# Two-map attention: no products of constants on TensorE, ScalarE's copy ahead of the next exponentials, a second pair of masked score tiles

## The reference, cut to what matters

```python
for l in range(DEPTH):                      # DEPTH = 2
    u = rmsnorm(x, norm1_g[l]) @ w_in[l]
    y_m = mlstm_mixer(...)                  # gated recurrence, all steps as one matrix
    y_a = diff_attention(...)               # the two-map attention
    y_h = hgrn2_mixer(...)                  # a second recurrence
    x = x + concat([y_m, y_a, y_h]) @ w_out[l]
    x = x + square(relu(rmsnorm(x, norm2_g[l]) @ w_up[l])) @ w_down[l]

def block(args):                            # 128 queries of the two-map attention
    s = einsum('bhcqd,bhckd->bhcqk', qi, kt)        # c: the two maps
    mask = qpos[:, None] >= kpos[None, :]
    p = softmax(where(mask, s, NEG_BIG), axis=-1)
    a = p[:, :, 0] - lam * p[:, :, 1]
    return einsum('bhqk,bhkv->bhqv', a, v)
```

## Time and profile before

| | |
|---|---|
| Median of 3 runs | 3468.72 us (3467.31 to 3468.8) |
| Profiled execution, its own time | 3470.07 us |
| Its span in the trace | 3468.3 us |
| Mean granted TensorE clock | 0.994 of full |
| TensorE matmul busy | 3410.0 us (98%) |
| VectorE busy | 1393.4 us (40%) |
| ScalarE busy | 1012.3 us (29%) |
| GpSimd busy | 1510.3 us (44%) |

### The profile page before, as it was taken

The page is one execution under the profiler, slowest core; times in us unless marked ns, Lnnn a source line. Parts: engine busy times, 40 slices in busy tenths (PEclk is TensorE's granted clock), DMA queues, the critical chain, the costliest instruction groups (busy, mean ns, idle before and its releaser), DMA issues.

```text
span 3468.3 us, 41846 instructions
## 1 busy us (share of the span) xinstructions
PE 3410.0 (98%) x16720; PEld 2748.6 (79%) x16720; DVE 1393.4 (40%) x2596; ACT 1012.3 (29%) x1275; POOL 1510.3 (44%) x522
## 2 busy tenths in 40 slices
PE   8999999899999999999999999999999999999999
PEld 7878878588888888886888887877888878778887
DVE  6565248735253524136312126854101158541010
ACT  2222322622223212224322233443212234442121
POOL 3545552035455545540354564502645545025453
PEclk9999999999999999999999999999999999999999
DMA  7444222024353443212222222201222212012222
GB/s 281 181 155 182 102 85 74 1 104 188 139 191 119 183 150 142 95 49 69 73 86 102 90 99 73 74 25 49 97 97 97 97 68 79 25 49 97 96 96 75
DMA packets 58748, 358.65 MB, mean 103 GB/s; under 512 B 10208, under 2 KB 10592, under 8 KB 21856
## 3 DMA queue, kind: packets, MB, share of 16 engines
q1 hardware_dynamic: 58592, 356.50, 28.6%
HBM read 354.38 MB, written 2.10 MB: 103 GB/s over the span
## 4 chain that ended last, share of the span: by engine, by line
PE 94%; DVE 3%; ACT 1%; issue 1%; DMA 1%; SPq 0%; POOL 0%; DVEq 0%; ACTq 0%
PE LP L572 85%; PE XB L572 8%; ACT E L1351 1%; DMA big<-w_ada 1%; PE LP L950 0%; PE XB L795 0%; DVE XB L2068 0%; PE XB L831 0%; ACT sq L1351 0%; DVE big L2248 0%; DVE big L2250 0%; DVE S L2424 0%; DVE big L2247 0%; DVE u L2909 0%; DVE h L2315 0%
## 5 line engine op out<-in xcount | busy, mean ns | idle before, releaser
L1855 POOL TENSOR_TENSOR w_lo<-ring,w_hi 128x2048 fp32r<-128x2048 f32 (+3 forms) x275 | 1134.4, 4125 | 700.0 <-ACT w_hi L1351 699.8
L572 PE MATMUL LP<-u_hi,w_hi 128*128 128x512 f32 x2448 | 959.5, 392 | 2.6 <-ACT u_hi L1351 2.4
L572 PE MATMUL LP<-u_hi,w_lo 128*128 128x512 f32 x2448 | 954.4, 390 | 0.0
L572 PE MATMUL LP<-u_lo,w_hi 128*128 128x512 f32 x2448 | 934.9, 391 | 0.0
L572 PE MATMUL LP<-big_r,w_hi 128*128 128x512 f32 x2520 | 780.3, 390 | 4.9 <-DVE h L2315 2.5
L1351 ACT ACTIVATE w_hi<-ring 128x2048 fp32r<-128x2048 f32 (+3 forms) x275 | 474.4, 1725 | 749.7 <-PE LP L572 746.8
L572 PE MATMUL LP<-big_r,w_lo 128*128 128x512 f32 x1508 | 587.5, 390 | 0.0
L572 PEld LDWEIGHTS LP<-big_r,w_hi 128*128 128x128 f32 x2520 | 472.6, 188 | 106.1 <-DVE h L2315 4.2
L572 PEld LDWEIGHTS LP<-u_hi,w_hi 128*128 128x128 f32 x2448 | 460.5, 188 | 111.6 <-issue 16.1
L572 PEld LDWEIGHTS LP<-u_lo,w_hi 128*128 128x128 f32 x2448 | 462.4, 189 | 96.2 <-issue 0.5
L572 PEld LDWEIGHTS LP<-u_hi,w_lo 128*128 128x128 f32 x2448 | 460.5, 188 | 95.8
(11 more groups left out here) (353 smaller groups left out, 3497.6 us busy)
## 6 DMA issues: line engine op xcount, KB each, us to landing
ada_in<-w_ada SPq DMA_DIRECT2D x66, 1024.0 KB, 4.9
ring<-w_in SPq DMA_DIRECT2D x20, 1024.0 KB, 4.8
ring<-w_gu00a SPq DMA_DIRECT2D x11, 1024.0 KB, 7.1
ring<-w_gu00b SPq DMA_DIRECT2D x11, 1024.0 KB, 6.6
ring<-w_gu01a SPq DMA_DIRECT2D x11, 1024.0 KB, 6.6
ring<-w_gu01b SPq DMA_DIRECT2D x11, 1024.0 KB, 6.7
ring<-w_gu10a SPq DMA_DIRECT2D x11, 1024.0 KB, 6.6
ring<-w_gu10b SPq DMA_DIRECT2D x11, 1024.0 KB, 4.9
```

Source lines behind the costliest of these rows:

```text
L572: return pe.matmul(o, lhsT=lhsT, rhs=rhs, start=start, stop=stop)
L1855: gp.tensor_tensor(w_lo[:, slab % RING, 0:width], ring[:, slab % RING, 0:width], w_high(q, width).bitcast(F32), ALU.subtract).then_inc(s(" ...
```

## The change

Four edits, all in the two-map attention.

- TensorE: `fill_heads` and its call go, 29 matmuls in each layer and their waits on `o_taken`.
- ScalarE: in step n the copy of unit n - 2 (`ET` from `XB[3]`) now stands ahead of the two exponentials of unit n. What `beside` does stays last.
- VectorE and ScalarE: odd units keep their masked scores in `big[:, HF:HF+2]` (two tiles that the recurrence has finished with) and not in `S`. So the mask of unit n waits for the exponentials of unit n - 2, not of unit n - 1.
- VectorE: one wait ahead of the pass, for its own last reads of `big[:, HF:HF+2]` (`x_ready`).

```diff
+        def diff_masked(n):
+            return big[:, HF:HF + 2, :] if n % 2 else S
...
-            def fill_heads(n, times):
-                if times and pl.head + n // NB > 1:
-                    pe.wait_ge(s("o_taken"), pl.head + n // NB - 1)
-                fill(times, LP[0][:, (pl.head + n // NB) % 2, :])
...
-                    fill_heads(n, {0: 5, 2: 5, 6: 2, 8: 2, 9: 3, 11: 2, 13: 3, 16: 5, 18: 2}.get(n, 0))
                     beside(n)
...
                 for n in range(n_units + 2):
+                    if n >= 2:
+                        i, W = n - 2, ((n - 2) % NB + 1) * P
+                        act.wait_ge(s("transposed"), p0 + i + 1)
+                        if i >= 2:
+                            act.wait_ge(s("pv_done"), p0 + i - 1)
+                        f(ET[:, i % 2, 0:W], XB[3][:, 0:W], ACT.Copy).then_inc(s("pt_done"), 1)
                     if n < n_units:
...
-                            f(E[:, k % 4, 0:W], S[:, m, 0:W], ACT.Exp, scale=-1.0, bias=stat[:, k % 4, 0:1],
+                            f(E[:, k % 4, 0:W], diff_masked(n)[:, m, 0:W], ACT.Exp, scale=-1.0, bias=stat[:, k % 4, 0:1],
                               accum_out=stat[:, k % 4, 1:2]).then_inc(s("diff_exp"), 1)
-                    if n >= 2:
-                        i, W = n - 2, ((n - 2) % NB + 1) * P
-                        act.wait_ge(s("transposed"), p0 + i + 1)
-                        if i >= 2:
-                            act.wait_ge(s("pv_done"), p0 + i - 1)
-                        f(ET[:, i % 2, 0:W], XB[3][:, 0:W], ACT.Copy).then_inc(s("pt_done"), 1)
                     beside(n)
...
-                            if n:
-                                dve.wait_ge(s("diff_exp"), u0 + k - 1)
+                            if n >= 2:
+                                dve.wait_ge(s("diff_exp"), u0 + k - 3)
                             dve.tensor_tensor_reduce(
-                                out=S[:, m, 0:W], in0=XB[k % 3][:, 0:W], in1=cc("causal", T - W, W), scale=1.0,
+                                out=diff_masked(n)[:, m, 0:W], in0=XB[k % 3][:, 0:W], in1=cc("causal", T - W, W), scale=1.0,
...
+                dve.wait_ge(s("x_ready"), 9 * (l + 1))
                 diff_attention(l, 2, st[:, 50 + l:51 + l], beside_maps)
```

## The result

The changed kernel takes 3479.99 us (median of 8 runs, 3475.69 to 3482.18) against 3468.76 before: ratio 1.0029, 95% interval 1.002 to 1.0039. It is slower by 11 us, clear of noise. It lies inside the range (3461 to 3482) but 7.5 us above the forecast, outside the forecast's own 3467 to 3478, and almost on case C's 3480.7.

What follows compares the result with a forecast made beforehand. TensorE, busy 98% of the span, was taken as the bound. Schedule -2.0 plus clock +3.9 gave +1.9 a pass, +3.8 in all: 3473.9 from the profiled execution, 3472.5 in terms of the runs' median; range 3461 to 3482.

Steps and rivals of the forecast that it cites:

- case C: Rival, slower: clock falls behind all five new spells, +8 a pass, ScalarE's queue passes it on; +12, 3480.7; chance 0.22.
- eight foretold waits: TensorE's idle spells in a pass once fills go: 1.75, 2.6, 0.66, 1.4, 1.57, 2.1, 1.9 and 2.85 us.
- n = 2: Second group of far products: TensorE idle 1.75 us for VectorE's copies, starting 2.95 us sooner than before.
- missing waits at n = 11 and 13: Sign against the forecast: TensorE should wait about 2 us each on ScalarE's gate copy there.
- "Nothing": Second pair of masked tiles: the freed wait ended last nowhere, so no gain; perhaps some tenths where ScalarE is late.
- The order of ScalarE: Exponentials of unit 9 behind the copy of unit 7 cost the queue to the gate copy 1.1 us.
- The gain of 0.4: n = 8: before, transposes waited 0.4 for a copy behind the exponentials of unit 7; the new order pays.
- Schedule alone: Waits without any clock effect: -2.0 us a pass, -4.0 in all, perhaps off by 1.5 a pass.
- The clock: Without fills, TensorE's clock falls three more times a pass at 1.3 us each: +3.9, between 0 and +8.
- is bound by TensorE again and moves with it: What follows the pass: no change of its own, it only shifts with the pass.
- B: Rival, the clock holds: spells under 2 us cost nothing, only the schedule counts; 3464.7, passes 59.7; chance 0.25.
- D: Rival, faster: new order and second tiles loosen the steps; 3455 with a steady clock, 3463 with falls; chance 0.08.

Runs made afterwards that it cites:

- experiment 1: The kernel before with its 29 products of constants a pass left out, nothing else changed: 3479.42 us, 1.0025 of before.
- changed kernel, fitted fills: The changed kernel given fills only as long as the wait each covers by the prediction's working: 3463.28 us, 0.9978 of before.
- fitted fills: The kernel before with fills resized to the waits of the prediction's working (none at n = 0, five at n = 4): 3463.96 us, 0.998 of before.
- the 3461 and 3463 kernels: Kernel before, resized fills, sums behind the pass spread among wide products, two fills there: 3461.19 us; resized fills alone in the kernel before, 3463.96, or changed kernel, 3463.28.

## Why the prediction was right or wrong, point by point

**The places and the releasers** were right in the main: of eight foretold waits (n = 2, 4, 6, 8, 9, 11, 13 and 16) the first pass has seven. At n = 11 it has none: TensorE, behind 10.2 us at half, was itself the last there. In the second pass, where that slow stretch is 6.8 us, the wait at n = 11 is there, 0.74 us. The prediction named missing waits at n = 11 and 13 as a sign that it is wrong; the first pass shows half of that sign. The sizes at 4, 6, 8, 9 and 16 were good to half a microsecond (2.14, 0.52, 1.47, 1.31 and 2.37); the two on the gate copy, forecast at 2.1 and 1.9, measured 0.74 at most and 0.80. The wait of 0.90 at n = 18, for ScalarE's copy, was not in the working.

**n = 2** was mis-sized: 2.88 us, not 1.75; the products start at t = 6.13, not 5.15. VectorE's second weights instruction took three times its length. Timelines of VectorE and of GpSimd:

```profile
2275.11 1.25 DVE L2396 SCALAR_TENSOR_TENSOR wk<-E,stat,wk 128x128 f32<-128x128 f32 x1
```

```profile
2274.95 1.26 POOL L2022 TENSOR_TENSOR Z<-Z,big 128x512 f32<-128x512 f32 x1
```

The Trainium skill (SBUF — State Buffer, "Who interferes with whom") has the rule: a VectorE instruction with two inputs in SBUF and a GpSimd instruction that reads SBUF share a port, and the later one waits for the whole of the other. The trace agrees: the instruction starts 0.16 us behind GpSimd's and ends 0.15 us behind it. Without fills and without the second pair of tiles (experiment 1) that instruction took 0.35 us, but the one ahead of it was held in its place. VectorE, GpSimd and TensorE there (the lines are numbered as in the kernel before):

```profile
2281.08 1.19 DVE L2396 TENSOR_SCALAR wk<-E,stat,st 128x128 f32<-128x128 f32 x1
```

```profile
2280.92 1.27 POOL L2025 TENSOR_TENSOR Z<-Z,big 128x512 f32<-128x512 f32 x1
```

```profile
2280.64 0.91 PE L572 MATMUL XB<-big 64*128 64x384 f32 x2 [0.62 <-DVE stat L2387]
...
2284.00 2.08 PE L572 MATMUL LP<-Z 64*128 64x256 f32 x8 [2.46 <-DVE wk L2856]
```

Behind a fill at n = 0 it takes 0.34. It reads one tile only, a case that the rule as told here does not cover. So the meeting with GpSimd's product comes with the missing fills at n = 0, not with the tiles. The tiles take away the wait of 0.62 us, and the products of n = 2 start at t = 6.13 with them and 6.45 without. "Nothing" was wrong for the tiles by 0.3 us a pass, a gain, in the kernels without a fill at n = 0 ("some tenths", as the prediction allowed), and right where the fills stand.

**The order of ScalarE**: the working gave it +1.1 us in the queue to the gate copy and a cost of about 1 us a pass. Measured 0.7 and 1.0 with all fills, and 1.3 at full clock with fitted ones, once the 0.31 of the tiles is counted apart. Right. The gain of 0.4 that I gave it at n = 8 isn't there: with the order alone the transposes still wait 0.4, for VectorE's weights.

**Schedule alone, -2.0 a pass**: 58.90 us at full clock (changed kernel, fitted fills) plus 1.5 for one slow stretch is 60.4, so -1.25. That is an estimate: no run has the changed kernel without fills at full clock. Off by 0.75, within the 1.5 allowed; the order and n = 2 are in it.

**The clock** is the term that was mis-sized. I took three more falls of 3.4 us each at 1.3, +3.9 a pass. The first pass has 27.3 us at half, 23.9 more than before, in five falls of 6.8, 3.4, 10.2, 3.4 and 3.4 us; the second has the same 27.3 in four. They cost 66.43 - 60.4 = +6.0. So there was more than twice the slow time that I had taken (10.2), and each 3.4 us of it cost less, 0.86 in place of 1.3. The link from waits to falls was wrong too. The wait of 2.37 at n = 16 has no fall behind it in the pass, and one fall begins with no wait near: from 2314.25 to 2317.70 TensorE is busy 3.38 of 3.45 us, on products of four rows among others, and then the clock is at half:

```profile
2314.25:2317.70 3.45, 3.38 (x12) 1.25 (x11) 3.19 (x9) 1.55 (x4) 0.00 (x0) 0.99 0.01 2
2317.70:2321.10 3.40, 3.40 (x16) 2.79 (x15) 1.86 (x8) 2.40 (x7) 0.00 (x0) 0.50 0.00 0
```

The reasoning that "a slow stretch makes TensorE busier and so shortens the next spell" is why I gave C only 0.22. Its first half held (n = 11 has no wait), but a shorter spell did not keep the clock up.

The sum of a pass is then -1.25 + 6.0 = +4.8, against +1.9. That is 9.6 of the 11 us. The rest is small and not shown to belong to the change: the stretch behind has 6.8 us at half instead of 3.4, +1.6 a layer, where I had nothing ("is bound by TensorE again and moves with it"). But the kernel with the tiles alone, whose passes are those of before, has 3.4 and 10.2 us at half in these two stretches, and the one with the order alone 3.4 and 6.8.

In the prediction's working, the waits that it lists add up to 14.8 us, not the 16 that it takes off for TensorE's busy share; its own 44.5 us of work would make that share 0.75, not 0.73. Nothing in the sum hangs on it.

**The rivals.** B fell (passes were to be 59.7), D too. C's signs were the ones seen: passes over 65 us, clock under 0.86. Its mechanism was half right: many falls, but some of them long, some not behind its spells, and 6.0 us a pass in place of 8. That its 3480.7 is 0.7 from the measured time is partly luck: the passes give 9.6 us of its 12. The section of the Trainium skill on short idling between groups (TensorE: Matmul & The Clock Gate, "A second HAM failure mode: psum-queue depth-cycling") spoke for C. This trace agrees on the swing: a pass with 12.6 us of idling in pieces under 3 us has five falls, one with 3.5 us has one. The clock's cost of 6.0 us is below those 12.6, but above the schedule's gain of 1.25.

**Open.** Why the stretch behind is slow for 3.4, 6.8 or 10.2 us in otherwise equal profiles (fitted fills: 10.2 and 6.8) was not settled. Nor was why each of the six kernels with five fills at n = 4 still shows a fall in one of its two passes, near n = 11 (40 to 43 us into the pass); nor which of the 3461 and 3463 kernels is the best.

## What to carry to other kernels

Before taking out work that only fills time on TensorE, list what each piece covers and price the clock for the whole stretch as well as the waits, past the end of the function edited: the falls did not stand behind the waits one by one. Read PEclk in windows beside the busy time, and do not take one-column products for fills: here they held the clock no better than waiting did. Where filling is kept, size it to the wait: here that was worth 0.2%, and 0.3% with the sums behind.

## What the runs showed of the hardware that was not expected

- The clock stayed at half for 10.2 us with TensorE busy 9.04 us of them, and was at half for 37.5 us of a pass in which TensorE idled 3.4 us and did one-column products in the fills' place.
- 3.4 us at half cost 1.55 us in the pass of before (61.68 against 60.13 us), and by the estimate above 0.86 each where the pass was full of waits.
- A VectorE instruction of 0.35 us took 1.25 beside a GpSimd product reading SBUF, and one of 0.34 took 1.19.
